# Sixteen attention steps written between the 24 projected blocks of the recurrent branch, in a decoder block on one core

## The chip, the cores and the metric

One core of a Trainium2 chip runs the whole program in one launch; the other cores are idle. The metric is the device time in microseconds, the median over several runs of the same kernel. Beside those runs there is one profiled execution, whose trace gives every duration quoted below.

## What is computed

The reference is one decoder block over 512 tokens of width 1024, in float32. Cut to what matters here:

```
h    = rms_norm(x) * (1 + scale1) + shift1            # [512, 1024]
proj = h @ w_in                                       # split into aq ak av | dq dk dv | dz | dbeta dalpha | gA gB
y_a  = sliding_window_attention(rms(aq), rms(ak), av, sinks) @ w_attn_branch
       # 16 heads, 4 key heads, window 128: per block of 128 queries, 256 keys, softmax with a sink
qkv  = silu(causal_conv4(concat(dq, dk, dv)))         # 24 blocks of 128 channels
beta = sigmoid(dbeta);  g = -exp(a_log) * softplus(dalpha + dt_bias)      # the decays
od   = gated_delta_rule(l2(q), l2(k), v, g, beta)     # chunks of 64 tokens, 8 heads
od   = rms_norm(od) * silu(dz)                        # the output gate z
y_b  = od @ w_dn_branch
x    = x + gate1 * ((sigmoid(gA)*y_a + sigmoid(gB)*y_b) @ w_out)
x    = x + gate2 * peer(rms_norm(x)*(1+scale2)+shift2)                    # table of 16384 experts
```

The modulation `mod = silu(c) @ w_ada + b_ada` gives the six shifts, scales and gates; two of them are needed before `h`, the other four (a weight of 1024 x 4096) later.

## The kernel before

Everything is kept transposed, channels on the 128 partitions and the 512 tokens along the free dimension. A weight comes as a slab of 256 columns (1 MB) through `Stream`: SyncE loads it, ScalarE copies it into a rounded high part (`pj_hi`, `split_hi`, L343), VectorE subtracts to get the low part (`pj_lo`, `split_lo`, L347), and TensorE multiplies each half slab, a block of 128 output channels, in 24 matmuls (L359 to L361: high by high, high by low, low by high, for 8 pieces of the 1024 rows). Each engine runs its own instruction list in order, and semaphores tie the lists together; nothing is scheduled at run time. The order of the lists is the order of the Python code, and each `nc.Block()` ends with all engines meeting.

The stages that the change touches, in the order in which they run:

- `phase_project`, 22 slabs. Slabs 0 to 5 give the queries and keys (12 blocks, copied out by ScalarE). Slabs 6 to 17 give the 24 blocks of the recurrent branch; for each, VectorE does the causal convolution straight from the result's bank (L536 and three times L539) and ScalarE the SiLU (L499). Slabs 18 to 21 give the output gate `z`, which ScalarE puts through SiLU (L507, L514). Then come the values and the two small columns per head (`av`, `ba`, four groups of matmuls, L472). Most of these lists are hardware loops (`Fori`). Beside all of it GpSimd works off `w_ada`: 16 chunks of 256 columns, each loaded by its own DMA (L437), multiplied by `silu_c` (L425), folded in two additions (L429) and a third into `ada_acc` (L433); TensorE sums `ada_acc` over partitions (L460) behind a slab.
- `phase_attend`, a block of its own. First the norms: squares on ScalarE (L682), sums on TensorE (L622, L626), then square roots and four reciprocals of 128 x 512 on VectorE (L728), scaled keys `kn`, and `qrs` per query. Then a loop over the 4 key heads, each with 4 steps of 128 queries. GpSimd stages the head's tiles (L610 to L612). A step is: scores on TensorE (L639), scale and mask on VectorE (L742), maximum (L746) and its small followers, exponentials on ScalarE (L693, L695), denominator (L754, L755) and division (L757) on VectorE, eight transposes on TensorE (`turn`, L649), copies on ScalarE (L702), the product with the values on TensorE (L660), a copy out on VectorE (L763).
- `phase_delta`. Before its loop it works out the decays: softplus and exponential by series, some 60 tiny VectorE instructions, two rounds of transposes on TensorE and two scans (L1033 to L1081). Its loop over 4 pieces of 128 tokens starts with GpSimd's copy `gs` (L857).
- `phase_mix`, 28 slabs: gate and branch slabs alternate for the attention (0 to 7) and the recurrent branch (8 to 15), then `w_out` (16 to 19) and the query projection of the expert table (20 to 27). The heads' norms (`heads`, `squares`, `mean`, `normed`) go along with slabs 0 to 6.

The long stage after these, `phase_peer`, is left as it is.

Of the kernel before, what the change touches and what calls it, by code (L numbers as in the profile page):

```python
# [365 lines left out]
def phase_project(nc, m, a, st):  # L366

    acc = [m.at(f"conv_acc{i}", [P, SEQ], 96 + 2 * i) for i in range(2)]  # L370
# [12 lines left out]
    ada_w = [m.at(f"ada_w{i}", [P, KC, SLAB], 176 + 8 * i) for i in range(2)]
    ada_acc = [m.at(f"ada_acc{i}", [P, SLAB], 124 + i) for i in range(2)]
    w_ada = a["w_ada"].rearrange("o (k p) n -> p (o k) n", p=P)
    ADA = 4 * D // SLAB
    s_ada_w = [m.sem(f"pj_ada_w{i}") for i in range(2)]
    s_ada_own, s_ada_acc, s_ada_sum = m.sem("pj_ada_own"), m.sem("pj_ada_acc"), m.sem("pj_ada_sum")
    v_raw = m.at("v_raw", [P, KC, NV], 192)
    v_hi = m.at("v_hi", [P, KC, NV], 64, F32R)  # L390
    v_lo = m.at("v_lo", [P, KC, NV], 64 + 9, F32R)

    with nc.Block() as block:
        @block.sync
        def _(sp):
            def cols(j):
                return w[:, :, bass.ds(j, SLAB)]
            every = slice(0, SLAB)

            for u in range(2):  # L400
                st.load(sp, 1, u, False, [(every, w[:, :, SLAB * (2 + u):SLAB * (3 + u)])])

            for u in range(2):
                kc = COL_K + 2 * HD * u
                st.load(sp, 2, u, False, [(slice(HD * d, HD * d + HD), w[:, :, kc + HD * (d // 2):kc + HD * (d // 2) + HD])
                                          for d in range(4)])

            with sp.Fori(DN // 2, N // 2) as i:
                for u in range(2):
                    at = sp.snap(i * (2 * SLAB) + (COL_DN - DN * SLAB + u * SLAB))  # L410
                    src = cols(at)
                    st.load(sp, i, u, False, [(every, src)])
            sp.dma_start(v_raw[:, :, 0:KVW], w[:, :, COL_V:COL_V + KVW]).then_inc(s_vload, 16)
            sp.dma_start(v_raw[:, :, KVW:NV], w[:, :, COL_BA:COL_BA + 16]).then_inc(s_vload, 16)

        @block.gpsimd
        def _(pool):

            c = Count(s_ada_own)
            nc.gpsimd.dma_start(ada_w[0][:], w_ada[:, :, 2 * D:2 * D + SLAB]).then_inc(s_ada_w[0], 16)  # L420
            nc.gpsimd.dma_start(ada_w[1][:], w_ada[:, :, 2 * D + SLAB:2 * D + 2 * SLAB]).then_inc(s_ada_w[1], 16)

            def chunk(i, u, first, last):
                pool.wait_ge(s_ada_w[u], i * 16 + 16)
                own(pool, c, nc.gpsimd.tensor_tensor(ada_w[u][:], ada_w[u][:], m.silu_c[:]  # L425
                                                     .rearrange("p (k o) -> p k o", o=1)
                                                     .to_broadcast([P, KC, SLAB]), ALU.mult))
# [11 lines left out]
            for u in range(2):
                chunk(0, u, True, False)  # L440
            n = c.n
            with pool.Fori(1, ADA // 2 - 1) as i:
                c.reg, c.per, c.n = i, n, 0
                for u in range(2):
                    chunk(i, u, False, False)
            c.reg, c.n = None, n * (ADA // 2 - 1)
            for u in range(2):
                chunk(ADA // 2 - 1, u, False, True)

        @block.tensor  # L450
        def _(pe):
            st.multiply(pe, 0, 0, m.h_hi, m.h_lo, True)
            st.multiply(pe, 1, 1, m.h_hi, m.h_lo, True)
            with pe.Fori(1, 1 + ADA // 2) as i:
                for u in range(2):
                    st.multiply(pe, u, i * 2 + u, m.h_hi, m.h_lo, False)

                    pe.wait_ge(s_ada_acc, i * 2 + (u - 1))
                    for half in range(SLAB_BLOCKS):
                        last = pe.matmul(m.bank[4][:, bass.ds(i * 4 + (2 * u + half - 4), 1)],  # L460
                                         ada_acc[u][:, P * half:P * half + P], m.ones[:, 0:1], start=True, stop=True)
                    last.then_inc(s_ada_sum, 1)
            with pe.Fori(1 + ADA // 2, N // 2) as i:
                for u in range(2):
                    st.multiply(pe, u, i * 2 + u, m.h_hi, m.h_lo, False)

            pe.wait_ge(s_vsplit, 2)
            pe.wait_ge(st.read, 2 * N)
            for t in range(NT):
                tok = slice(P * t, P * t + P)  # L470
                for n, (k, x, y) in enumerate(V_TERMS):
                    last = pe.matmul(m.bank[t][:, 0:NV], (m.h_hi, m.h_lo)[x][:, k, tok], (v_hi, v_lo)[y][:, k, :],  # L472
                                     start=(n == 0), stop=(n == len(V_TERMS) - 1))
                last.then_inc(s_v, 1)


        def loads(i, early):
            return 16 * (i + 1) if early else i * 16 + 16 * (1 + 3)

        @block.scalar  # L480
        def _(act):
            def copy_out(b, i, u, half, dst):
                act.wait_ge(st.ready, b)
                nc.scalar.activation(dst, m.bank[SLAB_BLOCKS * u + half][:], ACT.Copy).then_inc(st.read, 1)

            st.split_hi(act, 0, 0, 16, True)
            st.split_hi(act, 1, 1, 16, True)
            for s in range(DN):
                for half in range(2):
                    b = 2 * s + half  # L490
                    dst = m.aq[:, b, :] if s < AK else m.ak[:, b - 8, :]
                    copy_out(b + 1, 0, s % 2, half, dst)
                n = s + 2
                st.split_hi(act, n % 2, n, 16 * (n // 2 + 1) + (48 if n >= AK else 0), False)
            with act.Fori(DN // 2, Z // 2) as i:
                for u in range(2):
                    for half in range(2):
                        act.wait_ge(s_conv, i * 4 + (2 * u + half + 1 - 2 * DN))
                        nc.scalar.activation(m.dn[:, bass.ds(i * 4 + (2 * u + half - 2 * DN), 1), :]  # L499
                                             .rearrange("p o n -> p (o n)"), acc[half][:], ACT.Silu).then_inc(st.read, 1)  # L500
                    st.split_hi(act, u, i * 2 + (u + 2), i * 16 + 80, False)
            act.wait_ge(s_ada_acc, ADA)
            with act.Fori(Z // 2, N // 2 - 1) as i:
                for u in range(2):
                    for half in range(2):
                        act.wait_ge(st.ready, i * 4 + (2 * u + half + 1))
                        nc.scalar.activation(m.z[:, bass.ds(i * 4 + (2 * u + half - 2 * Z), 1), :]  # L507
                                             .rearrange("p o n -> p (o n)"), m.bank[2 * u + half][:],
                                             ACT.Silu).then_inc(st.read, 1)
                    st.split_hi(act, u, i * 2 + (u + 2), i * 16 + 80, False)  # L510
            for s in range(N - 2, N):
                for half in range(2):
                    act.wait_ge(st.ready, 2 * s + half + 1)
                    nc.scalar.activation(m.z[:, 2 * (s - Z) + half, :], m.bank[2 * (s % 2) + half][:],  # L514
                                         ACT.Silu).then_inc(st.read, 1)
            act.wait_ge(s_vload, 32)
            act.wait_ge(st.ready, 2 * N)
            nc.scalar.activation(v_hi[:], v_raw[:], ACT.Copy).then_inc(s_vsplit, 1)
            for t in range(NT):
# [664 lines left out]
def phase_mix(nc, m, a, st, slabs):  # L1184
# [26 lines left out]
    with nc.Block() as block:  # L1211
# [102 lines left out]
        def _(dve):  # L1314
# [734 lines left out]
```

## Time and profile before

| | us |
|---|---|
| median of 3 runs | 2794.13 (2793.66 to 2799.89) |
| profiled execution, its time | 2796.15 |
| its span in the trace | 2794.4 |
| `h` ready, `phase_project` begins | 94 |
| norms of attention begin | 377 |
| first step of attention | 411 |
| attention's last copy | 571 |
| first `gs` copy of the recurrence | 592 |
| `phase_mix` begins | 1031 |
| `phase_peer` begins | 1394 |

Times in the trace are counted from the start of the span. "Busy" is the sum of an engine's instructions; the granted clock of TensorE (PEclk) is a share of full speed, so that 1.00 is 2.4 GHz and 0.50 is 1.2 GHz, and values between are means over a stretch that had both. The numbers in the name of a line (L539) are lines of the kernel before unless said otherwise.

### The profile page before, as it was taken

How to read it: one execution, taken by the hardware profiler on the slowest of the kernel's cores; microseconds unless marked ns; L12 is line 12 of the kernel's file. 1: busy time of each engine (PE TensorE's matmuls, PEld its weight loads, DVE VectorE, ACT ScalarE, POOL GpSimd, SP SyncE). 2: the span in 40 equal slices, each digit the busy share in tenths (PEclk: the TensorE clock that was granted, in tenths of full speed). 3: DMA queues.
4: the chain of work that ended last, by engine and by line, in shares of the span. 5: the costliest groups of instructions: out<-in, count | busy, mean ns of one | idle time of the engine just before them, and what ended most of it. 6: DMA issues, size and time to landing. Idle time of an engine off the chain costs nothing.

```text
span 2794.4 us, 33600 instructions
## 1 busy us (share of the span) xinstructions
PE 2472.8 (88%) x12813; PEld 2084.0 (75%) x12813; DVE 1715.1 (61%) x3293; ACT 826.1 (30%) x1409; POOL 514.6 (18%) x453
## 2 busy tenths in 40 slices
PE   8799955548878779986989999969999999999998
PEld 7688854448778777874866668858888888888997
DVE  2457435444424437433189779947888878877666
ACT  1222223320120124322233334423333333333332
POOL 0599000010000000000000000123333333333210
PEclk7799966668868779998999999989999999999999
DMA  5455200000000012231133336788898888998762
GB/s 212 131 182 168 76 0 1 0 1 1 1 0 0 0 60 91 91 112 55 61 133 105 110 111 201 256 288 310 312 327 312 325 317 313 326 339 318 249 213 99
DMA packets 211924, 433.47 MB, mean 155 GB/s; under 512 B 21479, under 2 KB 127632, under 8 KB 211536
## 3 DMA queue, kind: packets, MB, share of 16 engines
q1 hardware_dynamic: 167104, 268.35, 28.5%
q0 software_dynamic: 44544, 161.24, 16.0%
q8 instruction: 85, 1.39, 0.2%
q10 hardware_dynamic: 144, 2.10, 0.2%
q14 instruction: 47, 0.39, 0.0%
HBM read 389.96 MB, written 41.68 MB: 154 GB/s over the span
## 4 chain that ended last, share of the span: by engine, by line
PE 47%; ACT 1%; DVE 1%; issue 1%; DMA 0%; POOL 0%; ACTq 0%; DVEq 0%; POOLq 0%
PE bank L1725 19%; PE bank L1616 10%; PE bank L1711 4%; PE bank L1709 4%; PE bank L1710 4%; PE bank L1680 3%; PE bank L1698 2%; PE bank L1602 1%; ACT ha L1761 1%; PE bank L1632 1%; DMA ug<-in_peer_u_dram,gidx 0%; DVE o_nat L2002 0%; DVE o_nat L2001 0%; ACT scores L1768 0%; DVE ug L1948 0%
## 5 line engine op out<-in xcount | busy, mean ns | idle before, releaser
L1616 PE MATMUL bank<-h2f,ua_T 128*128 128x384 f32 x832 | 297.7, 490 | 9.0 <-ACT ha L1761 9.0
L1725 PE MATMUL bank<-vt_hi,wg_hi 128*128 128x512 f32 x768 | 248.2, 404 | 3.8 <-DVE wg_lo L1992 3.6
L1725 PE MATMUL bank<-vt_lo,wg_hi 128*128 128x512 f32 x768 | 238.8, 392 | 0.0
L1725 PE MATMUL bank<-vt_hi,wg_lo 128*128 128x512 f32 x768 | 238.2, 391 | 0.0
L1709 PE MATMUL bank<-h_hi,uT_hi 128*128 128x384 f32 x608 | 210.7, 347 | 0.0
L1616 PEld LDWEIGHTS bank<-h2f,ua_T 128*128 128x128 f32 x832 | 145.7, 191 | 84.3 <-issue 16.7
L1974 DVE TENSOR_TENSOR vt_lo<-vt_raw,vt_hi 128x1024 fp32r<-128x1024 f32 x128 | 156.3, 1221 | 81.1 <-ACT vt_hi L1844 81.1
L1571 POOL DMA_INDIRECT ug<-in_peer_u_dram,gidx x128 | 142.7, 1115 | 344.0 <-DVE ug L1948 340.9
L1711 PE MATMUL bank<-h_hi,uT_lo 128*128 128x384 f32 x608 | 204.5, 336 | 0.0
L1710 PE MATMUL bank<-h_lo,uT_hi 128*128 128x384 f32 x608 | 203.9, 335 | 0.0
L1943 DVE TENSOR_TENSOR uT_lo<-bank,uT_hi 128x512 fp32r<-128x512 f32 x152 | 104.7, 689 | 134.1 <-ACT uT_hi L1829 134.1
L1576 POOL DMA_DIRECT2D hid_keep<-ha x52 | 28.3, 544 | 853.1 <-ACT ha L1761 853.1
L1589 POOL DMA_INDIRECT vg<-in_peer_v_dram,gidx x128 | 131.8, 1029 | 290.7 <-DVE g_acc L1963 275.6
L1829 ACT ACTIVATE uT_hi<-bank 128x512 fp32r<-128x512 f32 x152 | 90.4, 595 | 288.4 <-PE bank L1698 288.4
L1948 DVE SCALAR_TENSOR_TENSOR ug<-ug,h2n 128x1024 f32<-128x1024 f32 x128 | 155.6, 1218 | 25.7 <-DMA ug<-in_peer_u_dram,gidx 25.7
L1725 PEld LDWEIGHTS bank<-vt_hi,wg_lo 128*128 128x128 f32 x768 | 144.6, 188 | 31.8
L1725 PEld LDWEIGHTS bank<-vt_lo,wg_hi 128*128 128x128 f32 x768 | 144.6, 188 | 31.4
L1725 PEld LDWEIGHTS bank<-vt_hi,wg_hi 128*128 128x128 f32 x768 | 135.3, 189 | 39.9 <-issue 19.1
L1963 DVE SCALAR_TENSOR_TENSOR g_acc<-vg,g_hw,g_acc 128x1024 f32<-128x1024 f32 x127 | 162.5, 1279 | 1.1
L359 PE MATMUL bank<-h_hi,pj_hi 128*128 128x512 f32 x352 | 140.1, 398 | 22.7 <-DVE pj_lo L347 22.6
L1844 ACT ACTIVATE vt_hi<-vt_raw 128x1024 fp32r<-128x1024 f32 x128 | 135.0, 1055 | 80.3 <-PE bank L1725 80.3
L1855 ACT ACTIVATE wg_hi<-wt 128x384 fp32r<-128x384 f32 x128 | 67.3, 526 | 251.6 <-DVE wt L1987 251.6
(395 smaller groups left out, 5451.0 us busy)
## 6 DMA issues: line engine op xcount, KB each, us to landing
u_raw<-in_peer_u_dram SPq DMA_DIRECT2D x128, 512.0 KB, 5.9
vt_raw<-in_peer_v_dram SPq DMA_DIRECT2D x128, 512.0 KB, 5.9
gates<-g_stage SPq DMA_DIRECT2D x12, 2048.0 KB, 8.4
gate<-gates SPq DMA_DIRECT2D x32, 768.0 KB, 8.0
pj_raw<-in_w_in_dram SPq DMA_DIRECT2D x20, 1024.0 KB, 5.3
ada_w<-in_w_ada_dram POOLq DMA_DIRECT2D x16, 1024.0 KB, 5.6
hid_keep<-ha POOLq DMA_DIRECT2D x52, 192.0 KB, 2.1
hl<-hid_keep SPq DMA_DIRECT2D x52, 192.0 KB, 8.1
```

The costliest lines, as they stand in the source:

```text
L359: pe.matmul(self.m.bank[b][:], self.hi[u][:, k, cols], x_hi[:, k, :], start=(k == 0), stop=False)
L1571: nc.gpsimd.indirect_dma_start(ug[s % RING][:], None, u_rows, bass.IndirectOffsetOnAxis(m.gidx[:, s:s + 1].bitcast(U32), 0)).then_inc(s_ug ...
L1589: nc.gpsimd.indirect_dma_start(vg[e % RING][:], None, v_rows, bass.IndirectOffsetOnAxis(m.gidx[:, e:e + 1].bitcast(U32), 0)).then_inc(s_vg ...
L1616: last = pe.matmul(bank[6][:, 0:TD], uT[b % 2][:, k, :], m.h2f[:, k, P:], start=(k == 0), stop=(k == KC - 1))
L1709: pe.matmul(o, uT_hi[f % 2][:, k, :], m.h2_hi[:, k, P:], start=(k == 0), stop=False)
L1710: pe.matmul(o, uT_hi[f % 2][:, k, :], m.h2_lo[:, k, P:], start=False, stop=False)
L1711: last = pe.matmul(o, uT_lo[f % 2][:, k, :], m.h2_hi[:, k, P:], start=False, stop=(k == KC - 1))
L1725: ins = pe.matmul(y_bank[t][q][:], w[n % 2][:, tok], v[n % 2][:, 512 * q:512 * q + 512], start=(first and i == 0), stop=(last and i == 2))
L1844: nc.scalar.activation(v_hi[n % 2][:], v_raw[n % 4][:], ACT.Copy).then_inc(x["vhi"], 1)
L1948: v.scalar_tensor_tensor(ug[s % RING][:], ug[s % RING][:], 1.0, m.h2n[:], ALU.mult, ALU.mult, accum_out=h_raw[:, s:s + 1]).then_inc(x["dot ...
L1963: ins = v.scalar_tensor_tensor(acc[:], vg[s % RING][:], h_w[:, s:s + 1], acc[:], ALU.mult, ALU.add)
L1974: v.tensor_tensor(v_lo[n % 2][:], v_raw[n % 4][:], v_hi[n % 2][:].bitcast(F32), ALU.subtract)\
```

## The change

One written-out stage takes the place of `phase_project` and `phase_attend`; there are no hardware loops in it.

- The values are projected right behind the keys; the slabs of the recurrent branch come last, as 24 blocks into three rotating banks. The norms of attention stand among the values.
- The 16 steps of attention start at slots 2, 3, 4, 6, 7, 8, 10 and so on: `(4*i)//3 + 2`. A step is spread over four slots: scores, `soft` and exponentials in slot b, denominator and division in b+1, transposes in b+2, product and copy out in b+3. Each has one set of banks instead of two. The division by the denominator moves from VectorE to ScalarE (`scale`). The staging copies on GpSimd are gone, since TensorE reads `aq`, `kn` and `av` directly.
- The decays' preparation stands in the first three slots (`rates`, `decays`, `sums`; the exponential of `a_log`, `amplitude`, stands earlier), and is gone from `phase_delta`.
- `w_ada` goes in 32 chunks of 128 columns; TensorE sums chunk c at a fixed place (`ada_after`): chunks 0 to 9 behind blocks 2 to 11, two behind each of the four value groups, 18 to 22 in slots 0 to 4, the rest before the steps' products. Behind chunk 18 GpSimd also sets the scans' masks.
- The four slabs of `z` become the first four slabs of `phase_mix`.

In the diff the three long pieces are the lists of TensorE, of ScalarE and of VectorE, in this order.

```diff
+    at_score = {(4 * i) // 3 + 2: i for i in range(STEPS)}
+    SLOTS = BLOCKS + 2
+    ada_after = {c + 2: [c] for c in range(10)}
+    ada_after.update({12 + t: [10 + 2 * t, 11 + 2 * t] for t in range(NT)})
+    ada_after.update({16 + c - 18: [c] for c in range(18, 23)})
...
+            for s in range(DN):
+                for half in range(2):
+                    project(s, half)
+            pe.wait_ge(z["vsplit"], 2)
+            for t in range(NT):
+                values(t)
+                if t < 2:
+                    for n in range(6 * t, 6 * t + 6):
+                        squares(n)
+            for b in range(SLOTS + 2):
+                if b < BLOCKS:
+                    project(DN + b // 2, b % 2)
+                if b == 1:
+                    pe.wait_ge(z["gT"], 1)
...
+                if b - 2 in at_score:
+                    turn(at_score[b - 2])
+                if b - 3 in at_score:
+                    mixed(at_score[b - 3])
+                if b in at_score:
+                    scores(at_score[b])
...
+            for b in range(SLOTS + 2):
+                if b - 2 in at_score:
+                    turned(at_score[b - 2])
+                if b < BLOCKS:
+                    act.wait_ge(z["conv"], b + 1)
+                    nc.scalar.activation(m.dn[:, b, :], acc[b % 2][:], ACT.Silu).then_inc(st.read, 1)
+                    s = DN + b // 2
+                    if b % 2 and s + 2 < N:
+                        split(s + 2)
+                if b - 1 in at_score:
+                    scale(at_score[b - 1])
+                if b in at_score:
+                    exps(at_score[b])
...
+            for b in range(SLOTS + 2):
+                if b < BLOCKS:
+                    conv(b)
+                if b == 0:
+                    decays()
+                if b == 1:
+                    sums()
...
+                if b - 1 in at_score:
+                    denominator(at_score[b - 1])
+                if b - 3 in at_score:
+                    out(at_score[b - 3])
+                if b in at_score:
+                    soft(at_score[b])
...
-    slabs = []
+    slabs = [w_in[:, :, COL_Z + SLAB * i:COL_Z + SLAB * i + SLAB] for i in range(DNW // SLAB)]
...
-        phase_attend(nc, m, a)
```

The lists themselves, at the places of which the prediction speaks. TensorE before, in the attention loop of a key head (`sc` the scores, `pT` the transposed ones, `vs` and `ks` the staged tiles): only steps stand there.

```order
L639 MATMUL bank<-ks,qs 128x256 x8
L649 MATMUL bank<-ident,sc_1676 128x128 x8
L639 MATMUL bank<-ks,qs 128x256 x4
L660 MATMUL bank<-pT_1678,vs 64x128 x8
L649 MATMUL bank<-ident,sc_1677 128x128 x8
L639 MATMUL bank<-ks,qs 128x256 x4
L660 MATMUL bank<-pT_1679,vs 64x128 x8
```

TensorE now, at the end of block 5 and the start of block 6:

```order
L502 MATMUL bank<-h_hi,pj_hi_70 128x512
L503 MATMUL bank<-h_lo,pj_hi_70 128x512
L504 MATMUL bank<-h_hi,pj_lo_72 128x512
L554 MATMUL bank<-ident,sc_565 128x128 x8
L493 MATMUL bank<-ones,ada_acc_561 128x1
L568 MATMUL bank<-pT_566,av 64x128 x8
L502 MATMUL bank<-h_hi,pj_hi_71 128x512
```

Each group of a step now stands behind 24 matmuls of a block, and a chunk's sum stands ahead of the product. ScalarE before, in the loop over the recurrent branch's slabs (`dn` the SiLU of a convolution): two SiLUs and a high part in turn, one table load ahead of them in the loop.

```order
L499 ACT_TABLE_LOAD
L499 ACTIVATE dn<-conv_acc_549 128x512
L498 REGISTER_ALU
L499 ISA
L499 ACTIVATE dn<-conv_acc_550 128x512
L340 ISA
L342 ISA
L343 ACTIVATE pj_hi_70<-pj_raw_68 128x2048
```

ScalarE now, from the transposed copies of slot 4 to those of slot 5 and on to the division:

```order
L648 ACTIVATE pT_566<-bank 128x512 x2
L685 ACT_TABLE_LOAD
L685 ACTIVATE dn<-conv_acc_549 128x512
L640 ACTIVATE sc_565<-sc_565,es_575 128x256 x4
L632 ACT_TABLE_LOAD
L632 ACTIVATE sc_564,ssum_577<-sc_564,nm_571 128x256 x4
L634 ACTIVATE es_575<-sd_573 128x4
L648 ACTIVATE pT_567<-bank 128x512 x2
L685 ACT_TABLE_LOAD
L685 ACTIVATE dn<-conv_acc_550 128x512
L608 ACTIVATE pj_hi_70<-pj_raw_68 128x2048
L640 ACTIVATE sc_564<-sc_564,es_575 128x256 x4
```

The exponentials of a step have moved between two SiLUs, with a table load on either side. GpSimd before, one chunk of `w_ada`:

```order
L425 TENSOR_TENSOR ada_w_556<-ada_w_556,silu_c 128x2048
L429 TENSOR_TENSOR ada_w_556<-ada_w_556 128x1024
L429 TENSOR_TENSOR ada_w_556<-ada_w_556 128x512
L433 TENSOR_TENSOR ada_acc_558<-ada_w_556 128x256
L437 DMA ada_w_556<-in_w_ada_dram 128x8x256
```

GpSimd now, one chunk:

```order
L463 TENSOR_TENSOR ada_w_558<-ada_w_558,silu_c 128x1024
L467 TENSOR_TENSOR ada_w_558<-ada_w_558 128x512
L467 TENSOR_TENSOR ada_w_558<-ada_w_558 128x256
L471 TENSOR_TENSOR ada_acc_560<-ada_w_558 128x128
L456 DMA ada_w_558<-in_w_ada_dram 128x8x128
```

The same five instructions stand there, each over half the columns, and twice as many times.

## Rows read from the trace of the kernel before

**Rows 1.** Stretches: length, busy of PE, PEld, DVE, ACT, POOL; PEclk; DMA share, GB/s.

```profile
160.00:300.00 140.00, 137.88 (x629) 114.39 (x628) 97.77 (x97) 40.60 (x39) 117.00 (x53) 1.00 0.49 163
355.00:410.80 55.80, 34.41 (x200) 31.70 (x200) 22.93 (x18) 14.18 (x27) 0.77 (x2) 0.70 0.00 0
410.80:572.00 161.20, 86.87 (x512) 66.98 (x512) 79.83 (x224) 52.12 (x176) 8.39 (x12) 0.63 0.00 0
```

**Rows 2.** Waits, 376 to 592: engine and line, whom for, us, times, longest.

```profile
PE bank L649 <- DVE sc L757: 54.3, 12, 7.0
```

**Rows 3.** Timeline at attention's end and the recurrence's start.

```profile
571.07 0.42 DVE L763 COPY aq<-bank 128x256 f32 x1 [3.35 <-PE bank L660]
572.56 0.95 POOL L844 MEMSET states<- 128x1024 f32 x1 [38.91 <-POOLq L111]
...
591.81 0.19 POOL L857 COPY gs<-gcn 128x8 f32<-128x8 f32 x1 [17.49 <-DVE gcn L1081]
```

**Rows 4.** Timeline, two blocks of 24 matmuls end (ScalarE reads each).

```profile
1042.87 0.60 ACT L1260 ACTIVATE sig_a<-bank 128x512 f32<-128x512 f32 x1 [1.55 <-PE bank L361]
...
1048.31 0.60 ACT L1260 ACTIVATE sig_a<-bank 128x512 f32<-128x512 f32 x1 [4.84 <-PE bank L361]
```

**Rows 5.** Timeline of VectorE, the first convolution.

```profile
174.09 0.75 DVE L536 TENSOR_SCALAR conv_acc<-bank,colB 128x512 f32<-128x512 f32 x1 [1.22 <-PE bank L361]
174.87 2.32 DVE L539 SCALAR_TENSOR_TENSOR conv_acc<-bank,colB,conv_acc 128x511 f32<-128x511 f32 x3
```

**Rows 6.** Timeline of GpSimd, a full cycle of one chunk.

```profile
109.19 0.93 POOL L437 DMA_DIRECT2D ada_w<-in_w_ada_dram  x1 [0.30 <-POOL ada_acc L433]
...
120.64 0.92 POOL L437 DMA_DIRECT2D ada_w<-in_w_ada_dram  x1 [0.30 <-POOL ada_acc L433]
```

**Rows 7.** The page's DMA issues: count, KB each, us to landing.

```profile
ada_w<-in_w_ada_dram POOLq DMA_DIRECT2D x16, 1024.0 KB, 5.6
```

**Rows 8.** Groups by line: busy, mean ns, idle before.

```profile
L728 DVE RECIPROCAL krs<-krs 128x512 f32<-128x512 f32 x4 | 13.4, 3350 | 0.1
```

**Rows 9.** Timeline of TensorE in attention, one step's three groups.

```profile
474.66 1.70 PE L639 MATMUL bank<-ks,qs 64*128 64x256 f32 x8
476.30 1.15 PE L660 MATMUL bank<-pT,vs 128*64 128x128 f32 x16
...
481.37 1.09 PE L649 MATMUL bank<-ident,sc 128*128 128x128 f32 x8 [3.92 <-DVE sc L757]
```

**Rows 10.** Timeline of VectorE, the parts of a step.

```profile
476.54 1.66 DVE L742 SCALAR_TENSOR_TENSOR sc<-bank,qrs,amask 128x256 f32<-128x256 f32 x4 [3.50 <-PE bank L639]
...
479.68 0.16 DVE L749 TENSOR_TENSOR sd<-nm,nsink 128x4 f32<-128x4 f32 x1
...
479.95 0.18 DVE L755 RECIPROCAL es<-es 128x4 f32<-128x4 f32 x1
```

**Rows 11.** The low part's instruction: duration ns min/median/max, first and last start.

```profile
L347 DVE TENSOR_TENSOR pj_lo<-pj_raw,pj_hi x22: 2286/2575/6508, 96.2 to 333.0; 128x2048 fp32r<-128x2048 f32 x22
```

**Rows 12.** Timeline of ScalarE, exponentials from first to last, and transposed copies.

```profile
471.09 0.51 ACT L693 ACTIVATE sc<-sc,nm 128x256 f32<-128x256 f32 x1 [4.32 <-DVE sd L749]
...
473.07 0.19 ACT L695 ACTIVATE es<-sd 128x4 f32<-128x4 f32 x1
...
474.77 1.09 ACT L702 ACTIVATE pT<-bank 128x512 f32<-128x512 f32 x2 [1.51 <-PE bank L649]
```

**Rows 13.** The high part on ScalarE, by line.

```profile
L343 ACT ACTIVATE pj_hi<-pj_raw 128x2048 fp32r<-128x2048 f32 x22 | 41.8, 1904 | 1.9 <-PEq L167 1.9
```

**Rows 14.** Timeline of ScalarE, a switch of activation table.

```profile
574.10 1.28 ACT L990 ACT_TABLE_LOAD   x1
...
575.40 0.23 ACT L990 ACTIVATE dn_t<-dn_t 128x32 f32<-128x32 f32 x1
```

**Rows 15.** Timeline, the decays on VectorE: the start of `decays`, the end of the scans.

```profile
575.66 0.18 DVE L1040 TENSOR_SCALAR dn_t<-dn_t 128x32 f32<-128x32 f32 x1 [1.61 <-ACT dn_t L990]
...
580.25 0.19 DVE L1049 TENSOR_TENSOR g<-g,dn_t 128x32 f32<-128x32 f32 x1
```

More of the change, by code:

```diff
@@ L395, in _ @@
         def _(sp):
[L396 to L414, printed above, removed]
+            def slab(s):
+                if s < AK or s >= DN:
+                    c = SLAB * s if s < AK else COL_DN + SLAB * (s - DN)
+                    st.load(sp, s // 2, s % 2, s < 2, [(slice(0, SLAB), w[:, :, c:c + SLAB])])
+                else:
+                    c = COL_K + 2 * HD * (s - AK)
+                    st.load(sp, s // 2, s % 2, False,
+                            [(slice(HD * d, HD * d + HD), w[:, :, c + HD * (d // 2):c + HD * (d // 2) + HD])
+                             for d in range(4)])
@@ L439, in _ @@
[L439 to L448, printed above, removed]
+                    .then_inc(z["ada_acc"], 1)
+                if i + 2 < ADA:
+                    pool.wait_ge(z["ada_acc"], i + 1)
+                    load(i + 2)
@@ L453, in _ @@
[L453 to L469, printed above, removed]
+            def free(i):
+                if i >= 3:
+                    pe.wait_ge(st.read, i - 2)
+            def ada(c):
+                pe.wait_ge(z["ada_acc"], c + 1)
+                pe.matmul(O_BANK[:, ADA_COL + c:ADA_COL + c + 1], ada_acc[c % 2][:], m.ones[:, 0:1],
+                          start=True, stop=True).then_inc(z["ada_sum"], 1)
@@ new lines, in scores @@
+            def scores(i):
+                kv, n = divmod(i, NT)
+                if i == 0:
+                    pe.wait_ge(z["prep"], 1)
+                    pe.wait_ge(z["zero"], 2)
+                else:
+                    pe.wait_ge(z["soft"], i)
+                for h in range(2):
+                    rows = slice(HD * h, HD * h + HD)
+                    for b in range(2):
+                        last = pe.matmul(S_BANK[h][:, 2 * P * b:2 * P * b + 2 * P], m.aq[rows, 2 * kv + b, P * n:P * n + P],
+                                         kn[rows, kv, P * n:P * n + 2 * P], start=True, stop=True)
+                last.then_inc(z["score"], 1)
@@ L488, in _ @@
+            split(0)
+            split(1)
             for s in range(DN):
                 for half in range(2):
[L490 to L519, printed above, removed]
-                act.wait_ge(s_v, t + 1)
-                nc.scalar.activation(m.av[:, t + 1, :], m.bank[t][:, 0:KVW], ACT.Copy)
-                nc.scalar.activation(m.ba[:, t, :], m.bank[t][:, KVW:NV], ACT.Copy).then_inc(s_vread, 1)
+                    copy_out(2 * s + half)
```

689 lines of the change are left out of this document (339 added, 350 removed).

## Prediction

> **What bounds the kernel now.** I read the busy time by stretch first. From 160 to 300, among the projected blocks, TensorE is busy 137.9 of 140 us at a granted clock of 1.00, and VectorE 97.8 [rows 1]: TensorE sets the pace, and VectorE has a third of its time free. From 355 to 410.8 (values and attention's norms) TensorE is busy 34.4 of 55.8. From 410.8 to 572 (the 16 steps of attention) TensorE has 86.9, VectorE 79.8 and ScalarE 52.1 of 161.2 us, at a clock of 0.63: none is full, and a step takes 161.2 / 16 = 10.1 us. The waits say why: TensorE's transposes wait for VectorE's division 12 times, 54.3 us in all [rows 2]. A step is a chain through three engines, and only two steps are in flight. From the last copy at 571.5 to the recurrence's `gs` at 591.8 the core prepares decays [rows 3], mostly one small VectorE instruction after another. So some 200 us have no full engine, beside 140 us in which only TensorE is full.
>
> **What is moved out, at its price.** The four slabs of `z` are 8 blocks. A block costs 1048.31 - 1042.87 = 5.44 us of TensorE [rows 4], before as after, so `phase_mix` grows by 8 x 5.44 = 43.5 us. Nothing hides them: they stand ahead of the gate slabs on an engine that is full there. ScalarE and VectorE have per slab what they had (two SiLUs instead of two sigmoids, one high and one low part), well under 10.9 us. Against this the new stage ends without `z`.
>
> **The new stage, first part: to the end of the keys.** Unchanged: the first convolution starts at 174.09, when block 12 ends [rows 5], so the first 12 blocks end at 174.05 - 5.44 = 168.6.
>
> **Second part: values and norms.** TensorE's own work there is at most the 34.4 us of [rows 1], so it could be done at 203. But behind the fourth value group it waits for GpSimd's chunk 17, the eighteenth. A chunk of 256 columns took 120.64 - 109.19 = 11.45 us, of which 0.93 is the DMA's issue [rows 6]. The column work halves, the issue need not (the same 1024 pieces, half as long): 10.52 / 2 + 0.93 = 6.19 us. Bounds: 5.73 if the issue halves too, 7.1 if a further 0.9 us of fixed cost hides in the four instructions. With the first chunk started at 100.5, chunk 17 is done at 100.5 + 18 x 6.19 = 211.9. TensorE stands still for some 9 us in pieces of 2 to 5, which is a new wait, and I add 2.5 us for a lower clock behind it. Its loads are no bound: a buffer's load has 2 x 6.19 - 5.3 = 7.1 us, against 5.6 to landing for twice the size [rows 7]. Under the same cover VectorE does the four reciprocals, 13.4 us [rows 8]; with their followers they would end near 205. Were GpSimd fast, they would be the next thing late.
>
> **Third part: the lead-in, slots 0 to 4.** Behind block 0 (217.5) VectorE has the convolution, 177.19 - 174.09 = 3.10 us [rows 5], then `decays`, 580.44 - 575.66 = 4.8 us [rows 15] and one more product, 5.0. TensorE finishes block 1 at 223.7 and waits for them until 225.7: 2 us of the 20 stay exposed. The scans delay VectorE, not TensorE. Slots 2 to 4 take about 8 us each, with chunks 20 to 22 just in time. Block 4 ends near 248.
>
> **Fourth part: slots 5 to 23.** I wrote down what each engine has in four slots, in which three steps are started:
> - TensorE: 4 blocks of 5.44 and 3 steps. A step is 1.70 + 1.15 + 1.09 = 3.94 [rows 9]. Sum 33.6.
> - VectorE: 4 convolutions of 3.10; 3 x (3.30 for `soft` + 0.35 for the denominator, from [rows 10], + 0.42 for the copy out [rows 3]); 2 low parts of 2.58 [rows 11]. Sum 29.8. The division, which was here, is gone.
> - ScalarE: 4 SiLUs of 0.60 (a sigmoid of that form [rows 4]); 2 high parts of 1.90 [rows 13]; 3 x (exponentials 2.17 + copies 1.09 [rows 12] + division); 6 table switches of 1.30 [rows 14]. The division on ScalarE is not in the trace. It handles the elements of the two copies, so not under 1.09, and has four instructions like the exponentials, so not over 1.96; I take 1.5, the middle. Sum 28.3.
>
> TensorE has most, but the three nearly balance, and one handoff is late in each cycle. In slot b+1 of a step without scores (slots 5, 9, 13) ScalarE has in a row exponentials, copies, switch, SiLU, high part, division: 2.17 + 1.09 + 1.30 + 0.60 + 1.90 + 1.5 = 8.6 us after `soft`, and the transposes of the next slot wait about 1 us for it. Placing the instructions one after another with these durations, each at the latest of its waits, I get block 23 at 412.5, so 19 slots in 164.6, 34.65 per four. With the division at 1.1 or 1.96 the end moves by -2.6 or +5.8, with every low part at 5 us (the longest took 6.5 [rows 11]) by +17.
>
> **Last part.** Behind block 23: a convolution, and transposes, copies, product and copy out of the last step, 9 us: 421.7, with the 2.5 us from above 424.2. Then engines meet (572.56 - 571.49 = 1.07), GpSimd clears the states (0.95) and `gs` starts: 426.2. Before, it was 591.8 [rows 3].
>
> **Sum.** 591.8 - 426.2 = 165.6 earlier; less 43.5 in mixing: 122.1 us. The recurrence from `gs` to mixing and the whole last stage run the same lists. The profiled execution took 2796.15, 2 us over the median shown, so 2674 by it and 2672 by the median; I say **2674**.
>
> **Rivals.**
> - *TensorE sets the pace everywhere* (GpSimd 5.73 a chunk, handoffs hidden): 203, then 24 x 5.44 + 16 x 3.94 = 193.6 and 10 for decays and tail: 407, 17 us better, 2657. For it: TensorE has the largest sum. Against it: GpSimd has no free time in 160 to 300 but for its waits (117 of 140 busy [rows 1]).
> - *The table switches cost more than their load.* The stage has about 30 of them, where the recurrent loop had six. If each costs two loads, 2.6 us, ScalarE's sum per cycle is 28.3 + 7.8 = 36.1, it becomes the bound, and placing the list again gives 27 us more: 2701. Against it stands [rows 14]: load at 574.10 for 1.28, the next instruction at 575.40. The Trainium skill (ScalarE: Activation LUTs, "What ACT_TABLE_LOAD costs") says that a switch is the load of about 1283 ns and a drain of about 1380, some 2.66 us. By its figure the estimate would be 28 us more, near 2702. The trace shows the load's length and not the drain, and I go by the trace; but there the engine had nothing in flight, which in the new stage it may have.
> - *GpSimd is slower than half a chunk per chunk*, 7.1 us: it holds TensorE up through the values and into slot 5, 17 us more: 2691. For it: it has twice the instructions, waits and DMA issues.
> - *Steps and blocks do not overlap*: if each handoff misses its slot, a step costs its 10.1 us again beside the blocks: 212 + 131 + 162 + 9 = 514, 90 us more: 2764. Against it: each handoff has a whole slot, 8 us.
> - *Slower than before: TensorE's clock.* The steps ran at 0.63, and with gaps of 1 to 3 us in most slots the grant could fall to 1.2 GHz. 24 blocks at half speed are 131 us more, and 16 steps at what they took in attention (86.9 / 16 = 5.4 against 3.94 [rows 1, 9]) are 24 more: 155 us, 2829. It outweighs the gain once some four fifths of the slots run at 1.2 GHz. Against it: the blocks from 160 to 300 ran at 1.00, and TensorE is busy over 90% in this stage too, by my sums.
>
> **How the numbers follow.** Likeliest case, 2663 to 2687: 0.62. TensorE's pace 0.12, GpSimd 0.12, table switches 0.09, no overlap 0.02, clock 0.02, something else 0.01. The range 2650 to 2712 takes the first four but for their tails, some 0.85. A measurement here tells about 0.3%, 8 us, from no change. Only the clock, or two of the others at their worst together, come near that: faster 0.96, same 0.01, slower 0.03.
>
> **What would show it.** Right: `gs` near 426; 18 chunks of about 6.2 us on GpSimd, with TensorE waiting for `ada_acc` behind the value groups; blocks some 8.7 us apart from slot 5 on; a clock near 1.00 there; mixing 43 us longer; no table load followed by a gap. Wrong: blocks more than 9.5 us apart with TensorE waiting for `sc` from ScalarE (switches), chunks over 7 us, a granted clock under 0.9 in the slots, or a longer recurrence, which I hold unchanged.

## The result, and the profile after

The changed kernel takes **2697.4 us** (median of 4 runs, 2694.3 to 2700.7), the kernel before, on the same chip, 2793.9 (2793.5 to 2799.9): ratio 0.965, 95% interval 0.9632 to 0.9668. It is faster by 3.5%, where 2674 was forecast. Against the profiled execution of before (2796.15) the profiled one (2700.7, the slowest of the four, span 2698.6) gained 95.5 us, not 122.1.

`gs`, the line between the new stage and the recurrence, comes at 446.61 where before it was 591.81 [rows 3] and the forecast 426.2. So 20.4 of the missing 26.6 us lie ahead of it. The timeline at that place (start us, us, engine, line; the last copy out of attention, `gs`, and `gs` in the fourth iteration):

```profile
443.68 0.42 DVE L743 COPY aq<-bank 128x256 f32<-128x256 f32 x1 [6.92 <-PE bank L568]
...
446.61 0.19 POOL L903 COPY gs<-gcn 128x8 f32<-128x8 f32 x1
...
777.58 0.19 POOL L903 COPY gs<-gcn 128x8 f32 x1 [72.30 <-PE bank L1019]
```

Busy time by stretch of the changed kernel: the end of the keys, the values, slots 0 to 2, the slots behind them, the tail.

```profile
core 0: us, PE busy (x) PEld busy (x) DVE busy (x) ACT busy (x) POOL busy (x), PEclk, DMA share, GB/s
160.00:172.00 12.00, 7.59 (x36) 6.24 (x35) 11.49 (x16) 4.03 (x5) 10.89 (x11) 0.92 0.29 89
172.00:226.00 54.00, 45.04 (x236) 40.80 (x237) 35.87 (x21) 14.66 (x28) 49.08 (x45) 0.77 0.38 118
226.00:262.00 36.00, 21.73 (x97) 17.46 (x96) 33.02 (x47) 5.01 (x6) 25.20 (x23) 0.76 0.32 101
262.00:400.00 138.00, 130.33 (x775) 104.26 (x774) 113.65 (x192) 113.37 (x231) 42.89 (x40) 0.99 0.26 81
400.00:446.60 46.60, 37.94 (x236) 29.67 (x234) 30.23 (x59) 32.36 (x71) 0.88 (x1) 0.89 0.00 1
```

From 262 to 400 the stage is what was meant: TensorE 94% busy at a clock of 0.99, where attention had it at 54% and 0.63 [rows 1]. The odd stretch is 226 to 262: TensorE has 21.7 of 36 us, VectorE 33.0. TensorE's waits from 160 to 460 (total, times, longest):

```profile
PE bank L587 <- DVE g L767: 14.3, 1, 14.3
PE bank L554 <- ACT sc L640: 12.1, 7, 4.4
PE bank L493 <- POOL ada_acc L471: 8.1, 3, 4.4
PE bank L926 <- ACT dn_sq L1030: 7.4, 1, 7.4
PE bank L513 <- DVE v_lo L805: 5.2, 1, 5.2
```

The first is the wait for the decays, forecast at 2 us. VectorE's timeline there begins with `decays` in slot 0 and ends with its last product:

```profile
230.16 0.35 DVE L757 TENSOR_SCALAR dn_t<-dn_t 128x32 f32<-128x32 f32 x1
230.54 0.35 DVE L758 RECIPROCAL dn_t<-dn_t 128x32 f32<-128x32 f32 x1
230.93 2.75 DVE L759 TENSOR_TENSOR dn_t<-dn_t,dn_t 128x32 f32<-128x32 f32 x1
233.71 1.29 DVE L760 TENSOR_TENSOR dn_t<-dn_t 128x32 f32<-128x32 f32 x1
235.04 0.18 DVE L761 TENSOR_SCALAR g<-dn_t 128x32 f32<-128x32 f32 x1
235.25 0.59 DVE L763 TENSOR_TENSOR g<-g,dn_t 128x32 f32<-128x32 f32 x1
...
236.90 2.67 DVE L764 TENSOR_SCALAR g<-g 128x32 f32<-128x32 f32 x1
239.61 0.19 DVE L763 TENSOR_TENSOR g<-g,dn_t 128x32 f32<-128x32 f32 x1
...
246.92 0.19 DVE L767 TENSOR_TENSOR g<-g,na 128x32 f32<-128x32 f32 x1
```

And GpSimd's, with the same microseconds:

```profile
230.76 0.92 POOL L456 DMA_DIRECT2D ada_w<-in_w_ada_dram  x1 [0.30 <-POOL ada_acc L471]
231.71 1.91 POOL L463 TENSOR_TENSOR ada_w<-ada_w,silu_c 128x1024 f32<-128x1024 f32 x1
233.69 2.11 POOL L467 TENSOR_TENSOR ada_w<-ada_w 128x512 f32<-128x512 f32 x2
235.88 0.49 POOL L471 TENSOR_TENSOR ada_acc<-ada_w 128x128 f32<-128x128 f32 x1
236.67 0.92 POOL L456 DMA_DIRECT2D ada_w<-in_w_ada_dram  x1 [0.30 <-POOL ada_acc L471]
237.62 1.91 POOL L463 TENSOR_TENSOR ada_w<-ada_w,silu_c 128x1024 f32<-128x1024 f32 x1
```

Read them side by side. The instruction that starts at 230.93 ends at 233.68, when the multiplication does (231.71 + 1.91 = 233.62). The next takes 1.29, as long as the larger fold, 0.59 follows for the smaller, and 2.67 ends at 239.57, with the next multiplication (239.53). Each of the long ones seems to wait until one of GpSimd's ends, while those between them keep their 0.18 to 0.19. That is what all of them took undisturbed [rows 15], and so the whole of `decays`, 22 instructions, takes 16.95 us instead of 5.0. `amplitude`, ahead of `v_lo`, is stretched in the same way: its 31 instructions take 20.1 us (150.12 to 170.21) instead of 6.6 (as in no_gpsimd_math below). The experiments test this reading.

### The profile page after: what moved, and what is told of

Same layout as the page of the kernel before. It is cut to its first block, busy times and chain, and to the rows that moved or that the text cites. A ratio compares the mean times of both kernels' runs of the same rounds, so it can differ in the third digit from the quotient of the medians.

```text
span 2698.6 us, 33009 instructions
## 1 busy us (share of the span) xinstructions
PE 2453.7 (91%) x12813; PEld 2069.1 (77%) x12813; DVE 1720.4 (64%) x3229; ACT 885.1 (33%) x1500; POOL 519.7 (19%) x521
## 4 chain that ended last, share of the span: by engine, by line
PE 49%; ACT 1%; DVE 1%; issue 1%; DMA 0%; POOL 0%; ACTq 0%; DVEq 0%; POOLq 0%
PE bank L1721 20%; PE bank L1612 10%; PE bank L1707 4%; PE bank L1705 4%; PE bank L1706 4%; PE bank L1676 3%; PE bank L1694 2%; PE bank L1598 1%; ACT ha L1757 1%; PE bank L1628 1%; DMA ug<-in_peer_u_dram,gidx 0%; DVE o_nat L1998 0%; DVE o_nat L1997 0%; ACT scores L1764 0%; DVE ug L1944 0%
## 5 line engine op out<-in xcount | busy, mean ns | idle before, releaser
L1612 PEld LDWEIGHTS bank<-h2f,ua_T 128*128 128x128 f32 x832 | 145.5, 190 | 84.4 <-issue 16.7
L1721 PEld LDWEIGHTS bank<-vt_hi,wg_lo 128*128 128x128 f32 x768 | 144.5, 188 | 31.8
L347 DVE TENSOR_TENSOR mx_lo<-mx_raw,mx_hi 128x2048 fp32r<-128x2048 f32 x32 | 73.3, 2292 | 148.0 <-ACT mx_hi L343 148.0
L359 PE MATMUL bank<-h_hi,mx_hi 128*128 128x512 f32 x320 | 128.6, 402 | 26.4 <-DVE h_lo L1387 19.5
```

The source lines that it names most:

```text
L359: pe.matmul(self.m.bank[b][:], self.hi[u][:, k, cols], x_hi[:, k, :], start=(k == 0), stop=False)
L1612: last = pe.matmul(bank[6][:, 0:TD], uT[b % 2][:, k, :], m.h2f[:, k, P:], start=(k == 0), stop=(k == KC - 1))
L1721: ins = pe.matmul(y_bank[t][q][:], w[n % 2][:, tok], v[n % 2][:, 512 * q:512 * q + 512], start=(first and i == 0), stop=(last and i == 2))
```

## Experiments

Line numbers differ between kernels by a few. The table gives, from every trace, the start of the convolution of blocks 0, 1, 4 and 23 on VectorE, and `gs`; so it is free of what the recurrence scatters. The changed kernel stands there twice (changed_again is the same program on another chip, below called the repeat). Its two traces differ by 1.7 us in `gs` and by 1.3 us in the wait for the decays (14.3 and 13.0), so a difference of that size means nothing.

| kernel | block 0 | block 1 | block 4 | block 23 | `gs` |
|---|---|---|---|---|---|
| forecast | 217.5 | 225.7 | 248 | 412.5 | 426.2 |
| the change | 227.1 | 247.0 | 272.5 | 433.1 | 446.6 |
| changed_again | 227.7 | 246.3 | 272.1 | 431.3 | 444.9 |
| quiet_decays | 227.3 | 235.2 | 265.3 | 426.5 | 440.1 |
| decays_psum | 228.5 | 236.9 | 266.0 | 427.6 | 441.2 |
| spread_sums | 215.8 | 233.3 | 258.3 | 422.5 | 435.5 |
| spread_quiet | 213.7 | 221.6 | 251.7 | 417.8 | 431.2 |
| spread_quiet_early | 214.8 | 222.7 | 252.7 | 418.7 | 432.2 |
| early_amplitude | 228.1 | 247.2 | 272.5 | 433.1 | 446.7 |
| no_gpsimd_math | 209.7 | 217.8 | 241.6 | 401.2 | 414.7 |
| conv_copy | 227.0 | 244.0 | 269.9 | 422.0 | 435.5 |
| scale_before_split | 227.1 | 244.0 | 269.0 | 430.3 | 443.9 |
| division_vector | 228.3 | 246.9 | 277.2 | 441.4 | 453.3 |
| late_decays | 228.6 | 234.3 | 262.1 | 421.6 | 444.5 |

**GpSimd pauses (quiet_decays).**

```diff
+                if i == 19:
+                    pool.wait_ge(z["gT"], 1)
-    ada_after.update({16 + c - 18: [c] for c in range(18, 23)})
+    ada_after.update({16: [18]})
+    ada_after.update({c - 1: [c] for c in range(19, 23)})
```

> GpSimd waits before the arithmetic of chunk 19 until VectorE has finished the decays; TensorE takes up the sums of chunks 19 to 22 one slot later. Nothing is left out. Theory A (GpSimd's running chunks hold VectorE's small instructions): the decays fall from 17.0 us to about 5.0, as they took before the change; TensorE's wait for them falls from 14.3 us to some 2.5; `gs` comes at 434.6 instead of 446.6, and the time is 2685 us. Theory B (the small instructions are slow in this stage for a reason that has nothing to do with GpSimd, such as written-out code): the decays still take 15 to 17 us and the time stays at 2697, or rises by the 5 us for which GpSimd pauses.

Measured: 2692.7 us (2686.7 to 2694.4), ratio 0.9641 (0.9625 to 0.9657), an interval that still overlaps that of the changed kernel: the gain is read from the trace. The decays take 5.0 us (230.31 to 235.31) and TensorE's wait is 2.4 us, as theory A has it; B falls. But `gs` comes only 6.5 us earlier (4.8 against the repeat), not 12: block 1 is 11.8 us earlier, block 4 only 7.2. VectorE's timeline in slots 2 to 4 says where the rest went:

```profile
249.71 1.72 DVE L732 TENSOR_TENSOR nm<-nm,nsink 128x4 f32<-128x4 f32 x1
...
254.57 2.72 DVE L738 TENSOR_TENSOR es<-es,ssum 128x4 f32<-128x4 f32 x1
...
260.53 2.65 DVE L733 TENSOR_TENSOR sd<-nm,nsink 128x4 f32<-128x4 f32 x1
```

Three instructions of four columns, 0.16 undisturbed [rows 10], now meet the chunks that were put off, and hold VectorE 6.6 us.

**No arithmetic on GpSimd (no_gpsimd_math).** The multiplication and the two larger folds are taken out, so the modulation comes out as other numbers; the rest of each chunk stays.

> Leaves out the multiplication by the conditioning vector and the two larger folds of each chunk on GpSimd; loads, the last addition and all waits stay. This bounds what GpSimd costs the stage in all. Theory A: the amplitude takes 6 us instead of 20 and the values start near 168.6 (before: 172.8), the three waits for `ada_acc` (8.1 us) are gone, the decays take 5 us; together 4 + 8 + 12 = 24 us earlier, `gs` near 422, time near 2673. Theory C (only the pace of the chunks matters, the small instructions are slow by themselves): 8 us, 2689.

Measured: 2666.4 us, ratio 0.9537 (0.9521 to 0.9553), `gs` 414.74: 31.9 us earlier, more than the 24 I had counted. The mean of the amplitude's products falls from 832 to 185 ns and of `kn`'s product from 2418 to 752 ns. TensorE's waits from 160 to `gs` fall by 24.2 us (from 40.9 to 16.7), as counted. The surplus is the clock, which no sum of waits holds: for the same matmuls, from 160 to `gs`, TensorE is busy 235.1 instead of 242.6 us, at a mean clock of 0.95 instead of 0.90. The two make 31.8 of the 31.9 us. This trace also shows eight small instructions of VectorE beside an issue of a DMA by GpSimd with no multiplication behind it. They are hardly held; four of them:

```profile
216.34 0.90 POOL L456 DMA_DIRECT2D ada_w<-in_w_ada_dram  x1 [0.30 <-POOL ada_acc L465]
216.34 0.19 DVE L757 TENSOR_TENSOR g<-g,dn_t 128x32 f32<-128x32 f32 x1
216.57 0.18 DVE L758 TENSOR_SCALAR g<-g 128x32 f32<-128x32 f32 x1
216.79 0.19 DVE L757 TENSOR_TENSOR g<-g,dn_t 128x32 f32<-128x32 f32 x1
217.01 0.21 DVE L758 TENSOR_SCALAR g<-g 128x32 f32<-128x32 f32 x1
```

**The division ahead of the high part (scale_before_split).** `scale(...)` is moved above `split(s + 2)` in ScalarE's list.

> On ScalarE the division of a step's probabilities stands ahead of the high part of the next slab, not behind it. Nothing is left out. If the late handoff is what costs the slots (TensorE's transposes wait 12.1 us in seven places for `sc`), most of that goes: some 7 to 10 us, `gs` near 438, time near 2688. Rival: another handoff is late at once (the low part on VectorE, which follows the high part, or the convolution), and the time stays within 3 us of 2697.

Measured: 2700.4 us, ratio 0.9669 (0.9653 to 0.9685), no gain; `gs` 443.9. That is 2.7 us earlier (1.0 against the repeat), and the decays, for which TensorE waits 11.3 instead of 14.3 us here, account for all of it. The rival holds, as these waits show:

```profile
PE bank L587 <- DVE g L767: 11.3, 1, 11.3
PE bank L554 <- ACT sc L640: 10.2, 7, 4.4
...
PE bank L543 <- DVE sd L730: 3.5, 5, 1.7
```

What `sc` loses (1.9), `sd` takes (3.5).

**No table switches (conv_copy).** `ACT.Copy` for `ACT.Silu` behind the convolutions.

> The SiLU behind the convolutions is a plain copy, so that the recurrent branch gets other values; by that all table switches of the slots go, 33 of 1.3 us, 42 us of ScalarE. If a switch costs its load only and mostly lies beside TensorE's work, the slots get 5 to 12 us shorter (the handoff wait of 12.1 us), time 2685 to 2692. If a switch costs about as much again behind the load, the slots were bound by ScalarE and get 25 us shorter or more, time under 2675.

Measured: 2688.9 us, ratio 0.9625 (0.9609 to 0.9641). `gs` comes 11.1 us earlier (9.4 against the repeat), of which 3.0 (2.3) are again the decays: 7 to 8 us for 33 switches, 42 us of ScalarE. A slot takes (422.0 - 269.9) / 19 = 8.01 us instead of (433.1 - 272.5) / 19 = 8.45. So most of a switch lies beside TensorE.

**The amplitude in the conditioning stage (early_amplitude).** The call moves behind the product with `newton` in `phase_condition`.

> The amplitude of the decays, 30 small instructions of VectorE, stands in the conditioning stage, where GpSimd has no chunks, and no longer ahead of `v_lo`. Nothing is left out. Theory A: it takes 6 us there instead of 20, `v_lo` is ready when the keys end and TensorE's wait for it (5.2 us) goes. Of that only a part counts, since chunk 17 of GpSimd, done at 218, still ends the values: the three waits for `ada_acc` grow from 8.1 to 10 to 13 us, and `gs` comes 0 to 4 us earlier (443 to 447), less what the conditioning stage grows if its VectorE was not idle (0 to 6 us). If instead `v_lo` had set the end of the values, `gs` would come 5 us earlier by itself.

Measured: 2699.9 us, ratio 0.9648 (0.9624 to 0.9671), `gs` 446.67. Each of its instructions takes 0.17 us there, the wait for `v_lo` is gone, and the one for chunks has grown to 14.5, a little more than the 10 to 13 expected:

```profile
PE bank L514 <- POOL ada_acc L492: 14.5, 4, 5.2
```

Freeing one of two engines that end together gained nothing.

**One chunk sum per value group (spread_sums).**

```diff
-    ada_after.update({12 + t: [10 + 2 * t, 11 + 2 * t] for t in range(NT)})
-    ada_after.update({16 + c - 18: [c] for c in range(18, 23)})
+    ada_after.update({c + 2: [c] for c in range(10, 20)})
```

> TensorE takes up one chunk sum behind each of the four value groups instead of two; the four that are left over are spread over the later slots. Nothing is left out. Theory A: the values no longer wait for GpSimd (8.1 us gone) and end near 208 instead of 218; what is late next is VectorE, whose chain of reciprocals ended at 215.5, so the decays start 8 to 10 us earlier, still beside running chunks, and TensorE's wait for them stays 14 to 18 us. `gs` near 438, time near 2689. If GpSimd's pace was no bound, nothing changes.

Measured: 2690.3 us (2681.9 to 2691.0), ratio 0.9608 (0.9586 to 0.963), `gs` 435.5. Block 0 comes 11.4 us earlier and the chunk wait is gone. The wait for the decays is 12.0, below the 14 to 18 expected.

**The decays behind attention (late_decays).** `decays`, `sums` and the turning back stand behind the slots, with their tiles elsewhere.

> The decays, their prefix sums and the turning back stand behind the last step of attention, where GpSimd is quiet, in place of slots 0 to 2; the amplitude stays where it is. Theory A: the decays take 5 us there, and with transposes and prefix sums some 13 us lie open at the end; in exchange the 14.3 us wait in slot 1 goes. Together 0 to 4 us earlier, `gs` 442 to 447, time 2693 to 2698: preparing them in slot 0 has gained nothing. Theory B (small instructions are slow in the written-out code): 17 us for the decays here too, and `gs` some 10 us later, near 457.

Measured: 2700.3 us (2698.8 to 2701.4), ratio 0.9655 (0.9638 to 0.9671), `gs` 444.5. The decays take 5.0 us (432.29 to 437.28) in the same written-out code, so B falls a second time. Where the change prepares them is worth nothing by itself: the last copy ends at 432.37, not at 444.10, but from there to `gs` 12.2 us pass instead of 2.5. What is left, 2.1 us, is 0.3 against the repeat.

**The division back on VectorE (division_vector).**

> The division of the probabilities is back on VectorE, right behind the reciprocal, 4 x 349 ns a step as before the change instead of 4 x 493 ns on ScalarE. By my sums for four slots VectorE rises from 29.8 to 34.0 us, a little over TensorE's 33.6, so the slots should get 0 to 8 us longer; against it stands that the probabilities are ready earlier, and TensorE's waits for `sc` (12.1 us) go. I expect `gs` at 440 to 452, time 2691 to 2703. If VectorE as the bound outweighs it, convolutions are late and TensorE waits for free banks.

Measured: 2704.7 us, ratio 0.9664 (0.9647 to 0.9682), `gs` 453.3, 1.3 us outside the range I gave (the time 1.7). TensorE now waits 9.1 us for `sd` and 5.4 for `sc`. So of the change's parts the move of the division gave 6.7 us, read at `gs` (8.4 against the repeat); the intervals of the two ratios overlap and don't show it.

**Two remedies together (spread_quiet, spread_quiet_early)**, and the changed kernel again beside them:

> The changed kernel, unaltered, beside the two that follow and on the same chip: some 2697 us, `gs` between 443 and 447.

> The chunk sums spread over the stage and GpSimd quiet during the decays (its pause stands before chunk 15 here), the amplitude where the change has it. Nothing is left out. The spreading alone brought `gs` from 446.6 to 435.5 with 12.0 us of waiting for the decays left; the pause alone took 11.9 us off that wait and brought 6.5. Theory A: both together give the sum, `gs` at 429, time near 2681 by the changed kernel's 2697 with the recurrence as long as there.

> As the one before, and the amplitude in the conditioning stage. Theory A says that whichever of GpSimd and VectorE is later ends the values: by itself the early amplitude brought nothing, since TensorE then waited for chunk 17 (13.4 us in place of 8.1), but here the values no longer wait for chunks, so it should bring 4 to 5 us more: `gs` near 424, time near 2676. If parts simply add, it brings nothing here too: 429 and 2681.

Measured: 2696.3 us (2694.6 to 2701.7), 2686.3 (2684.4 to 2688.7) and 2682.3 (2680.6 to 2687.5); ratios 0.9649 (0.9634 to 0.9663), 0.9608 (0.9595 to 0.9621) and 0.9599 (0.9584 to 0.9614). Both beat the changed kernel, by 10 and 14 us, though less than expected: `gs` was to come at 429 and 424, and came at 431.2 and 432.2. The early amplitude brings no gain in `gs` here either: the values wait for chunks again, 4.3 us in two places. The 4 us between the medians are not resolved.

**The decays in PSUM (decays_psum).** GpSimd is not paused; only where the tiles lie differs.

```diff
+                view = lambda o: T_BANK[1][:, o:o + NT * DNH].rearrange("p (t h) -> p t h", t=NT)
+                tp, gp = view(0), view(NT * DNH)
-                    own(dve, c, v.tensor_tensor(g[:], g[:], t3[:], ALU.mult))
-                    own(dve, c, v.tensor_scalar(g[:], g[:], 2.0 / k, None, ALU.add))
+                    own(dve, c, v.tensor_tensor(gp, gp, t3[:], ALU.mult))
+                    own(dve, c, v.tensor_scalar(gp, gp, 2.0 / k, None, ALU.add))
```

> The running value of the series in the decays (`g` until its last product, and one temporary) lies in a free PSUM bank, so that only one of the 24 instructions still reads two tiles of SBUF and none scales one tile of SBUF into another; GpSimd keeps running beside them. Nothing is left out. In the traces so far the convolutions, which read PSUM, kept their 0.75 us beside GpSimd, while the decays' instructions each waited until a GpSimd instruction ended. If what is shared is an access to SBUF that only two-input and one-input forms on SBUF need (the Trainium skill, SBUF — State Buffer, states a lock of this kind), the decays take 6 to 9 us instead of 17 although GpSimd runs, TensorE's wait falls from 14.3 to 3 to 7 us, and `gs` comes near 437, 2 to 3 us before the version with the pause, since GpSimd loses nothing. If any small instruction of VectorE is held while GpSimd runs, the decays stay at 15 to 18 us and `gs` at 443 to 447.

Measured: 2690.4 us (2689.3 to 2691.6), ratio 0.9617 (0.9601 to 0.9633). VectorE's timeline from the first instruction of the decays to the scans behind them:

```profile
231.47 0.18 DVE L759 TENSOR_SCALAR bank<-dn_t 128x32 f32<-128x32 f32 x1
...
232.32 0.49 DVE L762 TENSOR_TENSOR dn_t<-dn_t 128x32 f32<-128x32 f32 x1
232.84 0.20 DVE L763 TENSOR_SCALAR bank<-dn_t 128x32 f32<-128x32 f32 x1
233.07 0.20 DVE L765 TENSOR_TENSOR bank<-bank,dn_t 128x32 f32<-128x32 f32 x1
...
236.80 0.19 DVE L769 TENSOR_TENSOR g<-bank,na 128x32 f32<-128x32 f32 x1
...
240.62 2.21 DVE L793 TENSOR_TENSOR_SCAN run<-keep,gT 8x512 f32<-8x512 f32 x1
242.87 1.11 DVE L794 TENSOR_TENSOR_SCAN off<-keep,run 8x32 f32<-8x32 f32 x1
```

GpSimd's timeline beside it:

```profile
232.29 0.46 POOL L471 TENSOR_TENSOR ada_acc<-ada_w 128x128 f32<-128x128 f32 x1
233.05 0.92 POOL L456 DMA_DIRECT2D ada_w<-in_w_ada_dram  x1 [0.30 <-POOL ada_acc L471]
234.00 1.91 POOL L463 TENSOR_TENSOR ada_w<-ada_w,silu_c 128x1024 f32<-128x1024 f32 x1
```

The decays take 5.5 us with GpSimd running. Of the 22 instructions (not 24, as expected above) only the one whose two inputs both lie in SBUF is held (0.49), and behind them the scans, which read two tiles. TensorE waits 2.8 us for the decays and 1.9 for the scans. So size and code are innocent: what is held is an instruction with two inputs in SBUF, or a small one-input one from SBUF to SBUF. `gs` is at 441.2, not 437: again the scans, and the small instructions of slots 2 to 4 (1.13 and 1.48 us), give back some 5 us. The Trainium skill (SBUF — State Buffer, section "SBUF: two separate sides") tells of an exclusive lock between VectorE and GpSimd, held for a whole instruction, for VectorE's forms with two SBUF inputs and its fast one-input modes. This trace agrees: 0.20 against 2.7 us for the same products.

## Why the prediction was right, and where it was off

Sign, size and range held (2650 to 2712); the forecast time was 23 us low, and the likeliest case (2663 to 2687) was missed. That the range held is in part luck. It had been drawn up to 2712 for a slower GpSimd (2691) and dearer table switches (2701). The second did not happen, the first only in part, and what did happen had no term in the sum. Against the forecast the trace is 9.6 us late at block 0, 21.3 at block 1, 24.5 at block 4, 20.6 at block 23 and 20.4 at `gs`. By its own steps:

- **The keys end at 168.6**: right within a microsecond (172.82 less a wait of 5.2). But the step went on at once to the values, and these began at 172.82, since `v_lo` came late. I had put no price on `amplitude` standing ahead of it on VectorE.
- **GpSimd's chunks, 6.19 us**: 5.87 undisturbed and 6.2 beside the reciprocals, so the halving was right. But five chunks took 7.1 to 10.6, each beside a low part of VectorE that held GpSimd (the longest, from 170.78 to 181.37, by `v_lo` and two low parts). The mean of the first 18 was 6.6, and chunk 17 was done at 218.0, not 211.9. The hold works in both directions. TensorE waited 8.1 us for chunks, as forecast (9).
- **Block 0, 5.6 us**: it took 9.1 (218.0 to 227.1). Behind the last wait for a chunk the clock was 0.50 until 224.2 and 1.00 after. The 2.5 us set aside for a lower clock belong here.
- **Decays, 5.0 us with 2 exposed**: this is the step that failed, 17 and 14.3. The duration came from [rows 15], where GpSimd stood still, and was carried to a place where it runs. The cost of an instruction depends on its neighbours. The longest low part of [rows 11], 6.51 us against a median of 2.58, had shown that in the trace of before, and I had read it only as a bound for low parts. There too the instruction ran on until GpSimd's multiplication ended, at 163.54, and then took some 2.2 us:

```profile
159.19 6.51 DVE L347 TENSOR_TENSOR pj_lo<-pj_raw,pj_hi 128x2048 fp32r<-128x2048 f32 x1 [9.09 <-ACT pj_hi L343]
159.92 3.62 POOL L425 TENSOR_TENSOR ada_w<-ada_w,silu_c 128x2048 f32<-128x2048 f32 x1
```

- **The lead-in, slots 2 to 4 in 22.3 us**: 25.4, so block 4 starts at 272.5 and not near 248.
- **Slots 5 to 23 in 34.65 us per four**: 33.8, 4 us better in all. TensorE had less to do than the sum of 33.6: it was busy 153.1 of 160.6 us, 32.2 per four slots. The late handoff cost more than I placed, 7.4 us of waiting for `sc` against 5. The division takes 1.69 us on ScalarE (1.5 taken).
- **Tail, 13.7 us from block 23 to `gs`**: 13.6, by luck. The forecast had 11.2 for the work and the 2.5 us for the clock, which was lost in block 0; the work took 2.4 more than forecast.
- **Recurrence unchanged**: the lists are the same, but `gs` to mixing took 444.1 against 439.3 us (in the repeat 1.8 longer than before). From the first `gs` to the fourth the traces of this study range from 327.6 to 334.8 us, before among them with 329.2: so I take it for scatter and not for the change, though a longer recurrence was among the signs of being wrong. **Mixing** grew by 43.8 (43.5), **peer** by 0.8.

20.4 + 4.8 + 0.3 + 0.8 make 26.3 of the 26.6 us. Of the rivals, *GpSimd is slower* named the right engine mostly for the wrong reason: not its own pace, but what it does to VectorE, and VectorE to it. The switches did not cost two loads each: in the slots too a load follows the instruction before it at once, and the next instruction the load,

```profile
273.32 1.05 ACT L648 ACTIVATE pT<-bank 128x512 f32<-128x512 f32 x2
274.39 1.28 ACT L685 ACT_TABLE_LOAD   x1
275.69 0.63 ACT L685 ACTIVATE dn<-conv_acc 128x512 f32<-128x512 f32 x1
```

and taking all 33 out brought 7 to 8 us. The Trainium skill (ScalarE: Activation LUTs, "What ACT_TABLE_LOAD costs") states a drain of about 1380 ns on top of the load. These rows do not bear it out.

## What to carry to other kernels

A duration read in a trace holds for its neighbourhood. Before small dependent instructions are moved under "free" time of VectorE, see whether GpSimd computes there: a small product between two SBUF tiles can then last until GpSimd's running instruction ends, here up to 2.75 us instead of 0.19. Put the running value in PSUM, or move GpSimd's work, and look at where that work lands, since it holds the next small instructions there.

## What the runs showed of the hardware

- VectorE's instructions with two inputs in SBUF (128 x 4 to 128 x 2048) and its small scalings, additions and casts from SBUF to SBUF are held beside GpSimd's arithmetic: those of 0.16 to 0.19 us took up to 2.75. With one operand in PSUM the same ones kept 0.20. Reciprocals of 128 x 512 from SBUF to SBUF kept their 3.35 us in every run.
- The hold begins before GpSimd's multiplication does: the instruction at 236.90 started 0.23 us into the issue of a DMA and ended with the multiplication that began at 237.62. The issue alone doesn't do it: in no_gpsimd_math, where no multiplication follows, the eight small instructions beside two issues took 0.17 to 0.29. Why the hold begins early is not shown.
- GpSimd is held as well: a pair of folds that takes 2.10 us took 4.06 beside a low part (148.12, low part from 147.20 to 150.20).
- Taking 24 us of waits from TensorE brought 32: its matmuls took 7.6 us less at the higher granted clock.
